# Moving the second stick-breaking pair, the key transposes, all heads and one merged transpose one or two slots later in a slot table

## What is computed

```
h = RMSNorm(x)
[pool | diff | stick-breaking | forgetting | gate logits] = h @ w_in      (1024 x 7428)
y_n = branch_n(...) @ w_branch rows of n                                  (four branches)
x = x + (sum_n sigmoid(gate_n + b_gate_n) * y_n) @ w_out
x = x + SwiGLU(RMSNorm(x))                                                (up 2 x 2816, down)
```

## Time and profile before

| | |
|---|---|
| median of 3 runs | 905.64 us (902.72 to 907.79) |
| span of the profiled execution | 905.8 us |
| TensorE busy | 889.5 us, 98% of the span |
| VectorE, ScalarE, GpSimd busy | 612.0, 443.4, 113.3 us |
| mean granted TensorE clock | 0.994 of full |

### The profile page before, as it was taken

One profiled execution on the slowest core, in us unless ns is written; L12 is line 12 of the kernel. 1 busy time (PEld: TensorE's weight loads), 2 busy tenths in 40 slices (PEclk: granted clock), 3 DMA queues, 4 the chain that ended last, 5 costly groups with the idle time before them and its releaser, 6 DMA issues.

```text
span 905.8 us, 11371 instructions
## 1 busy us (share of the span) xinstructions
PE 889.5 (98%) x4308; PEld 731.0 (81%) x4308; DVE 612.0 (68%) x902; ACT 443.4 (49%) x635; POOL 113.3 (13%) x89
## 2 busy tenths in 40 slices
PE   7998999999999999999999989999999999999998
PEld 6877888788878888888888878887887888888886
DVE  4989667676967666664478977668677676666542
ACT  5464635564345444443374645546544454444431
POOL 0534000000810010000005510000035000000000
PEclk9999999999999999999999999999999999999999
DMA  8744645565566766655655446464755566665551
GB/s 283 235 118 115 204 155 154 163 208 190 171 198 191 216 187 187 186 185 187 186 148 165 129 134 193 128 176 140 232 186 187 161 209 186 186 186 186 186 186 47
DMA packets 91014, 160.10 MB, mean 177 GB/s; under 512 B 11472, under 2 KB 17744, under 8 KB 90960
## 3 DMA queue, kind: packets, MB, share of 16 engines
q1 hardware_dynamic: 90960, 159.38, 57.4%
HBM read 158.31 MB, written 1.05 MB: 176 GB/s over the span
## 4 chain that ended last, share of the span: by engine, by line
PE 85%; DVE 10%; ACT 2%; issue 1%; POOL 1%; DMA 1%; POOLq 0%; SPq 0%; DVEq 0%; ACTq 0%
PE bulk L1576 25%; PE bulk L1580 25%; PE bulk L1577 25%; DVE w_lo L940 4%; PE bankAB L1337 1%; POOL wide L666 1%; PE bankT L1471 1%; DVE wide L1239 1%; PE bankAB L1338 1%; DMA raw<-in_w_in_dram 1%; PE bankAB L1339 1%; ACT w_hi L694 1%; PE bankAB L1517 1%; DVE stat L1026 1%; DVE wide L1038 1%
## 5 line engine op out<-in xcount | busy, mean ns | idle before, releaser
L940 DVE TENSOR_TENSOR w_lo<-raw,w_hi 128x1024 fp32r<-128x1024 f32 (+1 forms) x288 | 367.1, 1284 | 168.0 <-ACT w_hi L694 165.4
L694 ACT ACTIVATE w_hi<-raw 128x1024 fp32r<-128x1024 f32 (+1 forms) x288 | 299.9, 1048 | 265.3 <-PE bulk L1580 237.2
L1576 PE MATMUL bulk<-w_hi,hT_hi 128*128 128x512 f32 (+1 forms) x896 | 353.5, 395 | 3.0 <-DVE w_lo L940 2.8
L1577 PE MATMUL bulk<-w_lo,hT_hi 128*128 128x512 f32 (+1 forms) x896 | 346.7, 387 | 0.0
L1580 PE MATMUL bulk<-w_hi,hT_lo 128*128 128x512 f32 (+1 forms) x896 | 343.1, 387 | 0.0
L1576 PEld LDWEIGHTS bulk<-w_hi,hT_hi 128*128 128x128 f32 x896 | 169.3, 189 | 37.6 <-DVE w_lo L940 4.5
L1580 PEld LDWEIGHTS bulk<-w_hi,hT_lo 128*128 128x128 f32 x896 | 168.4, 188 | 34.4
L1577 PEld LDWEIGHTS bulk<-w_lo,hT_hi 128*128 128x128 f32 x896 | 169.2, 189 | 31.9
L1576 PE MATMUL bulk<-w_hi,aT_hi 128*128 128x512 f32 x176 | 69.9, 397 | 0.0
L1580 PE MATMUL bulk<-w_hi,aT_lo 128*128 128x512 f32 x176 | 69.6, 396 | 0.0
L1577 PE MATMUL bulk<-w_lo,aT_hi 128*128 128x512 f32 x176 | 69.6, 396 | 0.0
(11 more groups left out here) (234 smaller groups left out, 769.9 us busy)
## 6 DMA issues: line engine op xcount, KB each, us to landing
raw<-in_w_in_dram SPq DMA_DIRECT2D x112, 512.0 KB, 3.8
raw<-in_w_ffn_up_dram SPq DMA_DIRECT2D x80, 512.0 KB, 4.3
raw<-in_w_ffn_down_dram SPq DMA_DIRECT2D x44, 512.0 KB, 3.3
raw<-in_w_branch_dram SPq DMA_DIRECT2D x20, 512.0 KB, 3.4
raw<-in_w_out_dram SPq DMA_DIRECT2D x16, 512.0 KB, 3.3
bias<-in_b_gate_dram SPq DMA_DIRECT2D x16, 256.0 KB, 4.1
raw<-in_w_ffn_up_dram SPq DMA_DIRECT2D x16, 256.0 KB, 3.1
raw<-in_w_in_dram SPq DMA_DIRECT2D x8, 256.0 KB, 2.7
```

Of the source, the lines that this page charges most:

```text
L694: act.activation(w_hi[:, g % RING, :, 0:width], raw[:, g % RAW, :, 0:width], ACT.Copy).then_inc(hi_ready, 1)
L940: vec.tensor_tensor(w_lo[:, g % RING, :, 0:width], raw[:, g % RAW, :, 0:width], w_hi[:, g % RING, :, 0:width].bitcast(F32), ALU.subtract). ...
L1576: pe.matmul(dst, hi, whi, start=(k == ks[0]), stop=False)
L1577: pe.matmul(dst, hi, wlo, start=False, stop=False)
```

## The change

Only numbers in the two tables change; no instruction is added or removed by hand. `sb_sums`, `sb_weights`, `sb_out`, `sb_evac` of the second pair and the transposes of the differential keys go from slots 21 and 23 to 23 and 25. All eight heads and the fox transposes go two slots later. The second `tr_merged` goes one slot later. `cum` (31), `pool_a` (32), `pool_b` (34), `diff_norm` (46), `tr_diff` (50, 51), the gates and the sigmoids stay. TensorE's half of it:

```diff
-JOBS = [("diff", h, G0 - 3 + 3 * h) for h in range(4)] + [("fox", h, G0 + 10 + 2 * h) for h in range(4)]
+JOBS = [("diff", h, G0 - 1 + 3 * h) for h in range(4)] + [("fox", h, G0 + 12 + 2 * h) for h in range(4)]
...
-       (17, "sb_out", 0), (18, "sb_scores", 1), (21, "sb_sums", 1), (23, "sb_out", 1), (23, "tr_qk", "dk"),
-       (31, "cum"), (32, "pool_a"), (34, "pool_b"), (36, "tr_fox", "fq"), (37, "tr_fox", "fk")]
+       (17, "sb_out", 0), (18, "sb_scores", 1), (23, "sb_sums", 1), (25, "sb_out", 1), (25, "tr_qk", "dk"),
+       (31, "cum"), (32, "pool_a"), (34, "pool_b"), (38, "tr_fox", "fq"), (39, "tr_fox", "fk")]
...
-        (B0 + 8, "tr_merged", 0), (O0 + 2, "tr_merged", 1),
+        (B0 + 8, "tr_merged", 0), (O0 + 3, "tr_merged", 1),
```

More of the change, by code:

```diff
@@ L200 @@
        (12, "sb_logs", 0), (12, "sb_split", 0), (12, "qk_norm", "dk"), (14, "qk_evac", "dq"), (15, "sb_weights", 0),
-       (16, "svfq"), (17, "sb_evac", 0), (18, "sb_logs", 1), (18, "sb_split", 1), (20, "fkfv"), (21, "sb_weights", 1),
-       (23, "sb_evac", 1), (23, "qk_evac", "dk"), (24, "dv"),
+       (16, "svfq"), (17, "sb_evac", 0), (18, "sb_logs", 1), (18, "sb_split", 1), (20, "fkfv"), (23, "sb_weights", 1),
+       (24, "dv"), (25, "sb_evac", 1), (25, "qk_evac", "dk"),
        (28, "pf"), (29, "fox_forget"), (31, "cum_evac"), (32, "pool_evac_a"), (34, "pool_evac_b"),
-       (36, "fox_evac", "fq"), (37, "fox_evac", "fk")]
+       (38, "fox_evac", "fq"), (39, "fox_evac", "fk")]
 for _kind, _h, _s in JOBS:
@@ L215 @@
         _SV += [(LAST[("branch", _j, _n)] + 1, "branch", _j, _n)]
-_SV += [(B0 + 8, "merged_evac", 0), (O0 + 2, "merged_evac", 1),
+_SV += [(B0 + 8, "merged_evac", 0), (O0 + 3, "merged_evac", 1),
         (F0 - 3, "residual", "out", 0, 0), (F0 - 3, "gain", "ffn", 0, 0),
```

## The result

| | before | after |
|---|---|---|
| median of 20 runs | 907.07 us (902.72 to 909.91) | 910.0 us (905.13 to 914.52) |
| ratio, with its 95% interval | | 1.0034 [1.0019, 1.0049] |
| span of the profiled execution | 905.8 us | 905.0 us |
| mean granted clock of it | 0.994 | 0.996 |

The change makes the kernel about 0.3% slower in this series. The prediction said 903.6, and its range ended at 907.6. The profiled execution of the changed kernel is one of its quickest, and alone it would say that nothing was lost: spans of the 20 runs go from 903.3 to 912.7, and each time stands 1.7 to 2.8 us over its span.

What follows compares the result with a forecast made beforehand. TensorE, busy 98% of the span, was taken as the bound. Per layer 3.4 + 0.9 - 0.5 - 2.0 - 0.8 = +1.0 us, 2.0 for two: span 905.8 to 903.8, median 903.6 us, range 900.8 to 907.6.

Steps and rivals of the forecast that it cites:

- the old wait: TensorE's wait for `softplus_lo` at the second `sb_sums`: 2.43 us plus 1.65 of slow clock, 4.1 us a layer gained.
- the 0.5, 2.0 and 0.8 of the new ones: New bank T waits a layer: `cum` in slot 31, 0.5 us; `pool_b` in slot 34, 2.0; `tr_diff` in slot 50, 0.8.
- the 0.7 at unit 22: TensorE would wait about 0.7 us a layer for unit 22's `w_lo`, cutting the gain from 4.1 to 3.4.
- the function tables: Extra ScalarE table loads, costed at nothing; rival that they reach TensorE: 5.2 us more, 908.8, chance 0.03.
- GpSimd's wait: TensorE's wait at the second `tr_merged` for GpSimd's last addition of the gated sum: 0.9 us a layer gained.
- the main case: Waits change as summed and the clock does not fall again at slot 34: 903.6 us, chance 0.47.
- this one: Rival: the clock falls again behind slot 34's new wait, returning 1.65 us in each layer: 905.2 or 906.9, chance 0.32.
- the term put at nothing: Key transposes at slot 25, only two narrow units before head 0's scores: costed at nothing, 0.5 us if cover is gone.
- the prediction's own second case: The clock falls again behind the wait at slot 34, 1.65 us back a layer: 905.2 or 906.9, chance 0.32.

Runs made afterwards that it cites:

- sb22: Kernel before with only the second pair's `sb_sums` and `sb_weights` moved one slot later, 21 to 22: 899.77 us, ratio 0.9926.
- merged: Kernel before with only the second `tr_merged` and its evacuation one slot later: 903.16 us, ratio 0.9962 to the kernel before.
- pool_alone: Kernel before with only `pool_b` and its evacuation moved from slot 34 to 35, adding that bank T collision: 911.64 us, ratio 1.0047.
- sb_filled: Kernel before with 32 idle products on TensorE during the second pair's wait for `softplus_lo`: 905.36 us, ratio 0.9968.
- filled: Changed kernel with 26 idle products on TensorE between `pool_b` and head 1's `tr_probs` at slot 34: 906.80 us, ratio 0.9986 to the kernel before.
- after_again: Changed kernel run again in another series, no edit: 910.66 us (910.43 without an outlier), ratio 1.0033 to the kernel before.
- after_third: Changed kernel run a third time in another series, no edit: 907.07 us, ratio 1.0004 to the kernel before.
- pool_apart: Changed kernel with only `pool_b` and its evacuation moved to slot 35, out of its collision: 904.38 us, ratio 0.9964 to the kernel before.
- apart: Changed kernel with `cum` at 32, `pool_b` at 35, `tr_diff` of tile 0 at 51, evacuations too: 900.74 us, ratio 0.9923 to the kernel before.
- best: Kernel before with second `sb_sums` and second `tr_merged` one slot later each, heads unmoved: 895.52 us, ratio 0.9877.

## Why the prediction was wrong

**Right.** TensorE's waits decide, and all of them but one were named with their place and releaser. The gain of 4.1 us a layer for the old wait, in an execution where the clock falls behind it, is confirmed by the profile of sb22 (3.95), the 0.5, 2.0 and 0.8 of the new ones by the profile after, the 0.7 at unit 22 as well (84.32 - 83.28 - 0.24 = 0.80). No wait of TensorE shows the function tables. GpSimd's wait was worth 1.2 to 1.3 rather than 0.9.

**The step that failed** is the choice of the main case: "I give the main case, without the fall, 0.47 and this one 0.32." The old wait's fall was taken out in full, 1.65 us in each layer and every execution, and the new wait was given none. Neither holds. A wait of 2.3 us was followed by a fall in both layers of two profiles, in one of two layers of a third (merged), and in none of a fourth (pool_alone); one of 1.9 us was followed by a fall too, in some executions. The mean clock gives a first measure of how it stands overall: 0.9936, 0.9931 and 0.9936 in three series of the kernel before, and 0.9946, 0.994 and 0.996 in those of the changed one. That is a gain of about 1 us where 3.3 were booked, with the falls at the start counted in for both.

The spans give a second one, an estimate. From the mean span of the timed executions take the 449.0 us of rest, the mean start of the 13 profiles (70.5 us, the long one of sb_filled counted in) and two stretches without a fall (191.2 us each before, 192.6 changed; see below). What is left is 3.4 to 3.6 us for the kernel before in its three series; 3.3, 3.9 and 1.3 for the changed one; and nothing for filled. A fall took 1.5 to 1.8 us. So in the series of the result and of after_again falls of the clock, at slot 34 as filled shows, gave back the whole of what was booked for `sb_sums`, and in that of after_third a part of it. An error of half a microsecond in the mean start moves each of these figures by as much. The three profiles of the changed kernel show fewer falls, one in six such waits, than those two series would need; why is open.

**The second error is in the waits.** At equal clock the changed kernel is slower: executions at 0.996 have a mean span of 903.5 us before (10 of them, in the three series) and 906.7 after (15), those at 0.994 905.0 and 908.0. So the waits alone seem to cost 3.0 us, where the terms of the prediction without the clock give 2 x (-2.4 + 0.7 - 0.9 + 0.5 + 2.0 + 0.8) = 1.4. The stretches say nearly the same. Five layers of the changed kernel without a fall took 192.36 to 192.90 us, 192.6 on the mean. Before, a layer took 192.8 with its fall and about 191.2 without: from the second pair's scores to the first head's it took 27.24 us with the fall, and 25.60 in pool_alone without. That is 1.4 us a layer, 2.8 together. One part is the term put at nothing, the key transposes with only narrow units behind them. I had written that they "end about half a microsecond before they are needed". They end about there or after it: the first heads' scores waited 0.28 and 0.34 us in the first profile of the changed kernel, 0.50 and 0.36 in the second, nothing and 0.18 in the third, and 1.57 in layer 1 of pool_apart, where the clock then fell as well. ScalarE's timeline in that execution shows why:

```profile
538.14 1.06 ACT L694 ACTIVATE w_hi<-raw 128x1024 fp32r<-128x1024 f32 x1 [2.16 <-DMA raw<-in_w_in_dram]
539.11 0.36 ACT L698 ACTIVATE oT_hi<-bankO 128x256 fp32r<-128x256 f32 x1
539.37 1.08 ACT L755 ACTIVATE keys_hi<-bankAB 128x512 fp32r<-128x512 f32 x2
```

The evacuation of the keys now stands behind the rounding of unit 28, a full slab whose load lands late after the narrow ones, and by a different amount in each execution (ScalarE waited 2.16 us for it here, 0.88 in layer 0 of the first profile). The rest, about 1 us over the two layers, I could not assign; the changed table has one more slot in which TensorE breaks off its large products, and no run tests that.

**The third is the base.** The sum was set against a median of three runs, 905.64. With 20 runs it is 907.07, and a time stands some 1.8 us over its span. With that base and the clock's fall in both layers the prediction's own second case would have said 907.1 + 1.3 = 908.4 where 910.0 was measured; the 1.6 between them is about the size of the second error (1.4 to 1.6).

**Where the gain went.** Worth up to 4.1 + 1.3 us a layer, it was spent mostly on bank T: the heads moved onto the slots of stages that did not move with them. The rest, some 3 to 4 us, went to unit 22, the late heads and what is not assigned, as apart against best shows.

## What to carry to other kernels

When stages are shifted in an ordered table, list for every slot which buffers its stages write in sequence, and move the partners of a collision too; two writes to one bank in one slot cost the full chain of its readers (1.93 us here for ScalarE's and then VectorE's reading). Price a wait of the clocked engine with and without the fall of its clock, from more than one execution, and never book the fall's end as a sure gain while putting in a wait of nearly the same length. Cut the spans into parts before reading a mean clock: a part that the change does not touch, here the start, can lower it as well. Move as little as the wait needs: the second `sb_sums` and the second `tr_merged`, one slot later each, gave 1.2% here, and moving eight heads as well gave it back.

## What the hardware showed that I had not expected

The same wait, equal to the hundredth of a microsecond, is followed by a clock near half in one execution or layer and by full clock in another: 1.93 us at slot 34 (0.57 in layer 0 of after_again, 1.00 in both layers of the first profile). At `sb_sums` of merged the longer wait, 2.29 us, was followed by 1.00 and the shorter, 2.24 us, by 0.58. What decides between them is not shown by these runs. And products whose result nobody uses, in an idle bank, removed that loss: 26 of them at each of the two waits, some 1.6 us of work, made the changed kernel 3.6 us faster in the same series.
